# A hybrid transformer block in fp32 on one core: the latent tiles are turned beside the context tiles, and each layer opens with a plain fp32 product by token tile

## The reference, cut to what matters

```python
# first block, second ("odd") layer
h_l = rmsnorm(x, norm_g[l]) * (1 + sc_l[:, None]) + sh_l[:, None]
h_c = rmsnorm(ctx, norm_g[l]) * (1 + sc_c) + sh_c
q, k, v, g = split_cols(h_lat @ w_in, ODD_SPLITS)      # latents only for q and g
ck, cv = split_cols(h_ctx @ w_in[:, GQA_Q:GQA_Q + 2 * GQA_KV], ...)
...
# second block, each of two layers, 256 tokens, D = 1024
u = layer_norm(x) * (1 + sc1) + sh1
proj = u @ w_in + b_in
(p_in, c_b, c_c, c_h, mq, mk, mv, fq, fk, fv, f_logit, gate_logit) = jnp.split(proj, ...)
q_m = apply_partial_rotary(to_heads(mq, MOBA_HEADS), cos, sin)
k_m = apply_partial_rotary(to_heads(mk, MOBA_HEADS), cos, sin)
... # four branches, gates, w_o, layer norm, then the MLP w_up, relu^2, w_down
```

## Time and profile before

| | |
|---|---|
| time, median of 3 runs (range) | 1511.95 us (1504.79 to 1512.63) |
| the profiled execution: its time, its span | 1508.91 us, 1507.1 us |
| mean granted clock of TensorE | 0.955 |
| busy: PE, DVE, ACT, POOL | 90%, 64%, 33%, 10% |
| chain that ended last: PE, DVE, ACT | 74%, 15%, 4% |
| bytes from HBM, mean rate | 255.70 MB, 170 GB/s |

### The profile page before, as it was taken

How to read it: one execution, slowest core, us unless ns; L and a number is a source line. 1 busy time by engine, 2 the same in 40 slices (tenths; PEclk the granted TensorE clock), 3 DMA queues, 4 the chain that set the end, 5 groups by cost and what they waited for, 6 DMA issues and landing times.

```text
span 1507.1 us, 18982 instructions
## 1 busy us (share of the span) xinstructions
PE 1360.5 (90%) x7921; PEld 1115.3 (74%) x7921; DVE 963.0 (64%) x1231; ACT 501.0 (33%) x730; POOL 145.6 (10%) x163
## 2 busy tenths in 40 slices
PE   6999997897997888999998899995999999699996
PEld 1688754543795548888996898984988898598995
DVE  3657464753746875676678766667657677755556
ACT  1322134400434503352332433431453323334431
POOL 2011000100100010001222000001001132000000
PEclk9999999999999998998999899997999999899998
DMA  9353350321640057456565666655556476455551
GB/s 335 142 183 111 117 195 0 112 86 54 225 153 1 1 191 249 155 209 246 209 244 195 214 229 230 221 171 189 167 180 252 152 275 238 131 168 195 169 194 56
DMA packets 104918, 257.97 MB, mean 171 GB/s; under 512 B 8217, under 2 KB 11770, under 8 KB 104578
## 3 DMA queue, kind: packets, MB, share of 16 engines
q1 hardware_dynamic: 80554, 171.78, 33.3%
q0 software_dynamic: 20192, 75.58, 13.8%
q10 hardware_dynamic: 4088, 9.41, 1.9%
HBM read 255.70 MB, written 1.05 MB: 170 GB/s over the span
## 4 chain that ended last, share of the span: by engine, by line
PE 74%; DVE 15%; ACT 4%; issue 3%; ACTq 1%; DMA 1%; POOL 1%; SPq 0%; POOLq 0%; DVEq 0%
PE bank L729 72%; PE bank L875 2%; DVE weights_low L1951 2%; DVE modulation_sums L1769 1%; ACT weights_high L1403 1%; DMA x<-in_ctx_dram 1%; POOL inverse_roots L642 1%; ACT odd_prob L1577 1%; DVE statistics L1911 1%; DVE x L2373 1%; DVE even_A L1896 1%; DVE statistics L1809 1%; DVE x L1910 0%; DVE uT_high L2220 0%; DVE odd_weights_low L1951 0%
## 5 line engine op out<-in xcount | busy, mean ns | idle before, releaser
L1951 DVE TENSOR_TENSOR weights_low<-weight_ring,weights_high 128x2048 fp32r<-128x2048 f32 (+1 forms) x128 | 286.1, 2236 | 283.0 <-ACT weights_high L1403 282.9
L1403 ACT ACTIVATE weights_high<-weight_ring 128x2048 fp32r<-128x2048 f32 (+1 forms) x128 | 238.6, 1865 | 528.6 <-PE bank L729 453.9
L729 PE MATMUL bank<-uT_high,weights_high 128*128 128x256 f32 (+1 forms) x1200 | 346.6, 289 | 7.8 <-DVE weights_low L1951 3.0
L729 PE MATMUL bank<-uT_low,weights_high 128*128 128x256 f32 (+1 forms) x1200 | 344.3, 287 | 0.0
L729 PE MATMUL bank<-uT_high,weights_low 128*128 128x256 f32 (+1 forms) x1200 | 343.9, 287 | 0.0
L729 PEld LDWEIGHTS bank<-uT_high,weights_high 128*128 128x128 f32 (+1 forms) x1200 | 233.7, 195 | 12.8 <-issue 10.1
L729 PEld LDWEIGHTS bank<-uT_low,weights_high 128*128 128x128 f32 (+1 forms) x1200 | 233.7, 195 | 1.0
L729 PEld LDWEIGHTS bank<-uT_high,weights_low 128*128 128x128 f32 (+1 forms) x1200 | 233.6, 195 | 0.5
L1769 DVE SCALAR_TENSOR_TENSOR modulation_sums<-modulation_ring,silu_c_columns,modulation_sums 128x1024 f32<-128x1024 f32 x128 | 175.3, 1369 | 9.9 <-DMA modulation_ring<-in_w_ada_dram 6.9
L729 PE MATMUL bank<-weights_high,hidden_high 128*128 128x512 f32 x256 | 101.7, 397 | 5.2 <-DVE weights_low L1951 5.2
L729 PE MATMUL bank<-weights_low,hidden_high 128*128 128x512 f32 x256 | 101.2, 395 | 0.0
(11 more groups left out here) (287 smaller groups left out, 2168.1 us busy)
## 6 DMA issues: line engine op xcount, KB each, us to landing
weight_ring<-in_w_in_dram SPq DMA_DIRECT2D x52, 1024.0 KB, 6.5
modulation_ring<-in_w_ada_dram POOLq DMA_DIRECT2D x48, 1024.0 KB, 7.4
weight_ring<-in_w_up_dram SPq DMA_DIRECT2D x32, 1024.0 KB, 5.3
weight_ring<-in_w_down_dram SPq DMA_DIRECT2D x32, 1024.0 KB, 4.9
modulation_ring<-in_w_mod_dram POOLq DMA_DIRECT2D x16, 1024.0 KB, 5.4
weight_ring<-in_o_w_in_dram SPq DMA_DIRECT2D x10, 1024.0 KB, 5.1
weight_ring<-in_w_branch_dram SPq DMA_DIRECT2D x16, 512.0 KB, 3.6
weight_ring<-in_w_o_dram SPq DMA_DIRECT2D x8, 1024.0 KB, 6.9
```

The source lines that it names most:

```text
L729: return track(pe.matmul(*args, **kw))
L1403: act.activation(ring[:, s, 0:kn * cols], wring[:, slot, 0:kn * cols], ACT.Copy).then_inc(S["high_ready"], 1)
L1951: dve.tensor_tensor(lo[:, s, 0:kn * cols], wring[:, slot, 0:kn * cols], hi[:, s, 0:kn * cols].bitcast(F32), ALU.subtract).then_inc(w_free[ ...
```

## The change

Names are those of the diff; line numbers in the changed kernel differ by a few.

1. *Even output into odd layer.* A bank now holds two column blocks of one stream (latents or context). PE turns latent tile 0 after output tile 1 and latent tile 1 after output tile 2, all eight column blocks each; the context tiles are turned after `oq0`. DVE scales each tile right after its variance, splits the latent stream after tile 2, makes `oq0,1`, `oq1,0` and `oq1,1` low, then splits the context stream. ACT modulates the context stream after both halves of `oq1`. The temporary of the even output moves to another buffer.
2. *Layer start.* The slab order begins with `in2`, which is no longer split. Each token tile is turned and modulated by itself (8 turns, 8 modulations of 128 columns), and PE multiplies raw fp32 `whole` by raw fp32 `in2`, tile by tile. Then `in0`, `in1`, `in3`, `in4` as before. DVE rotates right after `in0`; in `in3` ACT makes the second half after two bank copies, and DVE puts its modulation product between the halves of `in4`.
3. *Small loads.* Bias rows, selectors, and for the second layer also biases and pool weights, are issued earlier: for the first layer after the odd attention, for the second inside the MLP of the first layer (after `high("up3")`).

```diff
-LAYER_SLABS = (halves("in0", "in1", "in2", "in3", "in4", "forget")
+LAYER_SLABS = (halves("in2", "in0", "in1", "in3", "in4", "forget")
-SPLIT_SLABS = [s for s in LAYER_SLABS if s[0][:6] != "branch"]
+SPLIT_SLABS = [s for s in LAYER_SLABS if s[0][:6] != "branch" and s[0] != "in2"]
-        etmp = E3[:, 0:2 * COLS].rearrange("p (b n) -> p b n", b=2)
+        etmp = acc1[:, 0, :].rearrange("p (b n) -> p b n", b=2)
...  PE, even output into odd layer
             tokens_out_by_tile(both("eout1"), [("eout", 1, i) for i in range(TALL)], eyT_tokens,
-                               between=lambda i: turn_tile(i - 1) if i > 0 else None)
-            turn_tile(TALL - 1)
-            turn_x("oxT", xn_o, range(4, KD), 2 * TALL)
+                               between=lambda i: turn_tile(i - 1, turned) if 1 <= i <= TC else None)
...
+            tokens_out(both("oq0"), [("oq", 0, i) for i in range(TC)], h_tokens, COLS, wait=h_split(0))
+            turned = [start(("oxT", 4 + n)) for n in range(4)]
+            for i in range(TC, TALL):
+                turn_tile(i, turned)
+            tokens_out(both("oq1"), [("oq", 1, i) for i in range(TC)], h_tokens, COLS)
+            tokens_out(both("okv"), [("okv", i) for i in range(TALL)], h_tokens, COLS, wait=h_split(1))
...  PE, layer start
-                turn_xn("xT", 0)
+                def first_tile(o, tt, h):
+
+                    w = slab("in2", h)
+                    copied(("xT", tt, h))
+                    for k in range(4):
+                        ins = product(o[:, :], whole[:, 4 * h + k, P * tt:P * tt + P], w[:, k, :],
+                                      start=(h + k == 0), stop=(h == 1 and k == 3))
...
+                turn_tile(0)
+                firsts = [start(("mqk", tt)) for tt in range(TC)]
+                first_tile(firsts[0], 0, 0)
+                turn_tile(1)
+                first_tile(firsts[0], 0, 1)
+                for h in range(2):
+                    first_tile(firsts[1], 1, h)
-                tokens_out(both("in2"), [("mqk", i) for i in range(TC)], ui, COLS)
...  ACT, even output into odd layer
-            act.wait_ge(S["xn_ready"], 2 * TALL)
-            modulate("oxT", whole_o, (2, 3), range(4))
+            modulate_stream(0)
             high_part("oq0", 1)
-            modulate("oxT", whole_o, (2, 3), range(4, KD))
-            high("oq1", "okv", "og0")
+            high("oq1")
+            modulate_stream(1)
+            high("okv", "og0")
...  ACT, layer start and inside the MLP
+                for tt in range(TC):
+                    for b in range(2):
+                        o = ready(("xT", tt, b))
+                        for n in range(4):
+                            k = 4 * b + n
+                            ins = act.activation(whole[:, k, P * tt:P * tt + P], o[:, P * n:P * n + P], ACT.Identity,
+                                                 bias=mcol[:, 0, k:k + 1], scale=mcol[:, 1, k:k + 1])
+                        release(ins, ("xT", tt, b))
+                    if tt == 0:
+                        act.wait_ge(S["x_out"], sec.at("x_out", 0))
+                        if l == 0:
+                            load_biases(l)
+                high("in0")
+                if l == 0:
+                    load_pools(l)
+                else:
+                    load_pool_matrices()
+                load_norm(l, 1)
...
+                    if j == 2 and not sec.last:
+                        load_rows(l + 1)
+                        load_selectors()
+                        load_biases(l + 1)
+                        load_pools(l + 1)
...  DVE, even output into odd layer
+                normal_o(i)
+                if i == 0:
+                    low("oq0", 0)
+                if i == TC:
+                    split_stream(0)
+            low("oq0", 1)
+            low("oq1")
+            split_stream(1)
...  DVE, first layer start: mod_columns(7, mcol, 1) moved ahead of normal(0, 8)
...  DVE, layer start
-                low("in0", 0)
-                for i in range(4):
-                    copied(("xT", i))
-                    split_u(i)
-                low("in0", 1)
-                low("in1", 0)
+                for tt in range(TC):
+                    for b in range(2):
+                        copied(("xT", tt, b))
+                        src, hi, lo = (v[:, 4 * b:4 * b + 4, P * tt:P * tt + P] for v in (whole, uhigh, ulow))
+                        link(dve.tensor_copy(hi, src))
+                        dve.tensor_tensor(lo, src, hi.bitcast(F32), ALU.subtract).then_inc(S["u_ready"], 1)
+                low("in0")
```

201 lines of the change are left out of this document (113 added, 88 removed).

## The result

Four runs each on the chip: the kernel before took 1512.29 us in the median (1504.79 to 1517.05), the changed kernel 1487.26 us (1481.72 to 1489.12). The ratio is 0.983, with a 95% interval of 0.980 to 0.985. The forecast was 1480 with a range of 1470 to 1494. The profiled execution of the changed kernel took 1481.7 us with a span of 1479.9, against 1508.9 and 1507.1 before: 27.2 us less, where the prediction's sum was 28.9. It was the fastest of the four.

The account below looks back on a forecast made before the run. Three quarters of the chain was PE at work, so only PE's idle, low-clock or needlessly dear stretches counted. From the profiled 1508.9 us, -13 - 7.3 - 9.0 + 0.4 = -28.9 gave 1480 us, range 1470 to 1494.

Parts of the forecast that it names:

- (A): Odd layer: waits for scaled tiles go, two low-part waits come, `okv` begins at 395.5 instead of 408.4, -13 us.
- rival 1: Odd layer: the new pauses of 2.6 and 2.4 us cool the clock, 2.1 us each, 1484 us; chance 0.12.
- (B): First hybrid layer's start: plain products by tile begin at 562.5 instead of 572.7, `in2` falls away later, -7.3 us.
- (C): Second hybrid layer's start: plain products begin at 1035.5, -9.0 us, more than in the first layer since loads stand elsewhere.
- The step that named the fourth half-slab as just in time: First hybrid layer: `in0,1` is low at 585.0, PE wants it at 585.2; nothing to spare, nothing lost.
- The wait at `in4`: Layer starts: PE's wait for DVE before the first `in4` product falls from 1.5 to 0.4 us, -1.1.
- The price of the restart: Layer starts: PE runs 4 us at the low clock after restarting, which loses 2.0 us.
- (D): First layer's MLP: fifteen small loads delay the rounding of `down2,0`, cost 0 to 2.7 us, taken as +0.4.
- The upper bound: First layer's MLP: cost of 2.7 us if the loads start only when the rounding is over.
- Rival 2: Layer starts: the fourth half-slab comes late, 5.7 us more in each layer, 1491 us; chance 0.11.
- Rival 3: Odd layer: each new wait doubles (+5) and the restart cools, odd part -6, 1487 us; chance 0.09.
- Rival 4: Every restart: clock stays low until dense split products come, +16.6 us, 1525 us; chance 0.04.

Follow-up runs that it names:

- odd part alone: The kernel before with only the odd layer's part of the change, layer starts and small loads as they were: 1499.7 us, ratio 0.992.
- six traces: Traces of six kernels that have the changed kernel's code at the second layer's start, which took 90.3 to 92.1 us, 91.4 in the mean.
- the second trace: The changed kernel measured again, unaltered, beside the others on one chip: 1488.7 us, ratio 0.983.
- the experiment: The changed kernel with the last two half products of tile 1 swapped, so `in2,0` stays in use 3.4 us longer: 1496.7 us (1 run).
- loads alone: The kernel before with only its small loads moved off the layer starts, ten still ahead of the first layer's modulation: 1503.6 us, ratio 0.994.
- `oq0,1` edit: The changed kernel with the low part of `oq0,1` made on DVE ahead of the last tile's normalisation: 1489.1 us (1 run).
- four edits: The changed kernel with `okv,0` and `oq0,1` low parts earlier, MLP loads spread, second layer's tile 0 normalised earlier: 1476.5 us, ratio 0.976.
- layer part alone: The changed kernel with the odd layer's part taken back to what it was: 1498.5 us, ratio 0.991.
- `in2` split: The changed kernel with the first product by token tile done in three split passes instead of plain: 1497.3 us, ratio 0.990.

## Why the prediction came out as it did

**(A) Odd layer, -13 forecast; `okv` began 10.7 us earlier (11.1 counted from the output product).** The steps held: the waits for `odd_xn` went, and two for the low parts came, forecast 2.6 and 2.4, measured 2.36 and 3.12. From the end of `oq0,1` on (381.7) DVE's queue ran as forecast: low part of `oq1,1`, four splits, rotations, low part of `okv,0`. PE was 0.3 us quicker than forecast over its turns and two half-slabs, and starts 0.25 after the low part ends, so the second wait is longer. What was missing is the clock, at 1.7 us for the one low stretch of that trace; rival 1 had put 2.1 on each pause. The odd part alone, whose clock did not fall before `okv`, began that block 12.6 us earlier than before, counted the same way: the 12.9 of the forecast. The gain itself is not clock: on the chain 1.7 us were lost to it before and 1.7 after, and the 11 us are waits and work.

**(B) -7.3 forecast, -7.4 from `okv` to the first scores (-7.6 from the last output product); (C) -9.0 forecast, -8.8, or -7.7 by the mean of six traces.** (B) had the right size; (C) came as near only in the shortest trace, and the forecast is 1.3 us too high against the mean. The step that named the fourth half-slab as just in time was right to the tenth. The forecast start of the first product, 562.5 less 12.9, gives 549.6; it was 551.7, as (A) was short by 2.2. The wait at `in4` went altogether, where 0.4 was forecast. The low clock at the first restart lay on 5 us of plain products, not 4. The forecast did not say which part earns how much; the loads and the order by tile turned out nearly equal. Why (C) exceeds (B) was put down to the loads: they do give 1.3 us more there, but what is left over besides loads and order gives 1.2 less, and by the mean (C) hardly exceeds (B).

The price of the restart was right, but its reason was misread. The prediction took the low clock after 572.7 for what the sixteen turns at 564 had left as it was. The clock had in fact risen at 566.6, and fell again at 570.0, while PE waited 4.2 us for the split (the row of the turns, then windows):

```profile
563.89 3.25 PE L875 MATMUL bank<-constants,xn 128*128 128x128 f32 x16
564.00:566.00 2.00, 2.00 (x11) 2.00 (x11) 1.91 (x3) 1.09 (x1) 1.71 (x3) 0.50 0.89 364
566.00:567.00 1.00, 1.00 (x8) 0.90 (x6) 1.00 (x1) 0.00 (x0) 0.91 (x2) 0.70 0.61 150
569.00:570.00 1.00, 0.00 (x0) 0.00 (x0) 0.00 (x0) 0.00 (x0) 0.00 (x0) 1.00 0.92 282
570.00:571.00 1.00, 0.00 (x0) 0.00 (x0) 0.00 (x0) 0.62 (x2) 0.00 (x0) 0.51 1.00 381
```

**(D) +0.4 forecast, +0.8 measured,** and 0.1 in the second trace. The fifteen issues took 7.5 us (7.7 forecast, from 9.75 us over 19 loads; the trace of before has 18). The upper bound, in which they start only when the rounding is over, does not occur: the first went out 0.01 us after the rounding began.

**The sum** was made against one profiled execution, 3 us under the median then shown, and came out 1.7 us from the profiled execution of the changed kernel. That it is so near is partly luck: (A) fell 2.2 us short, and the profiled execution was the fastest of its four. Medians are 25.0 apart, not 27.2 or 28.9. The last 2.7 us of the traces' difference lie in the second layer's gate phases, which the change does not touch: there the clock was lower in the trace of before than in that of after. The same two blocks of branch products took 25.04 us at a mean clock of 0.86 and 20.29 at 0.83 in the kernel before. In the changed kernel:

```profile
1127.48:1151.09 23.61, 23.61 (x155) 20.18 (x154) 13.10 (x20) 8.35 (x18) 2.91 (x4) 0.93 0.54 201
1151.74:1170.57 18.83, 18.83 (x136) 17.43 (x136) 13.52 (x19) 4.22 (x11) 3.97 (x4) 0.91 0.68 251
```

In the first layer it went the other way: 197.2 against 195.7. This is chance, not an effect of the change.

One thing the sum had no term for: over whole runs the low clock shrank. A run's time multiplied by 1 less its mean granted clock is 73.9 us in the mean of eleven runs of the kernel before and 62.0 in six of the changed one, 11.9 us less of some 25. A part of it falls where PE waits or is off the chain, and lengthens nothing.

**The rivals.** *Rival 1* (the pauses cool the clock) is what happened, by half in the first trace and whole in the second, at 1.7 us each. *Rival 2* (the slab late) did not happen in the first trace; its premise, no slack, is shown by the experiment, and its price was set too low, for the clock comes on top. In four other traces the second layer's slab landed in 5.5 to 6.5 us and PE waited 0.5 to 1.6 us for it; in three a later slab took some 13 us beside ACT's 2 MB of constants and norm rows, for a wait of 0.5 to 0.8. *Rival 3* (DVE holds back the odd layer) fell: the pauses were not twice as long. *Rival 4* (the clock stays low until dense split products come) fell. The clock was back at 1.0 by 557, under the plain products of tile 0:

```profile
551.00:553.00 2.00, 1.28 (x2) 0.79 (x3) 1.91 (x5) 1.98 (x6) 0.18 (x1) 0.50 0.43 103
...
555.00:557.00 2.00, 2.00 (x4) 0.82 (x3) 1.93 (x4) 0.00 (x0) 1.56 (x3) 0.57 0.23 35
557.00:559.00 2.00, 2.00 (x12) 1.26 (x11) 0.86 (x2) 0.65 (x2) 0.00 (x0) 1.00 0.92 309
```

The turns of tile 1 at 557.71 did not bring the low clock back. The rule that the prediction took from the Trainium skill ("TensorE: Matmul & The Clock Gate", Part 4: PE-mode transpose) says that turns do not bring the full clock as other work does. The kernel before shows otherwise: there the clock rose at 566.6, when PE had done one product of one column (from 563.44) and then only turns (from 563.89). It rose likewise under the sixteen turns in the odd part alone (at 560.7) and in *loads alone* (at 574.2).

## What to carry to other kernels

Where a stage starts with operands that must be prepared on two engines, look for one product that can run on what is there already, in a dearer form: here 16 plain fp32 products took 2.9 us more than 48 split ones and opened an order worth some 3.2 at each start, because they need neither rounded weights nor the second token tile. Small loads at a stage start are worth moving by themselves: taking 8 of 18 issues in the first layer and 15 in the second off ACT's queue there gave 3.4 and 4.7 us. And when a wait goes, read the queue of the engine that releases the next one: two moves on DVE's queue alone, seen only in the new trace, took a further 5 us.

## What the runs showed of the hardware

**The length of a pause did not decide whether the clock fell.** The pause before `oq0,1` (2.3 to 2.4 us) stood in eight traces; behind it PEclk fell to 0.5 in five. The one before `okv,0` (3.1 to 3.2 us) stood in eight; the clock fell behind it in six. In five traces it fell behind one of the two alone. Of nine pauses of 3.53 us in the three kernels that keep the odd layer of before, seven went with a fall. A low stretch of the odd layer took away 1.7 us of full clock each time, or 3.4 where it lasted twice as long (less where PE was waiting anyway), and could begin inside dense products behind pauses of 0.7 and 0.95 us alone, as near 341 us in the kernel with the `oq0,1` edit and in the one with all four. An expected gain from "no pause, no low clock" is therefore an average, and one trace is a poor witness for it; the means of six runs each, 62.0 us lost in the changed kernel and 56.9 with the four edits, are a better one.

**The spread of whole runs is largely this.** The gate phases of layer 1 took 191.4 to 198.8 us in thirteen traces of the same code; in two at the ends of that range (the layer part alone and `in2` split), the clock's loss, counted as in the ledger, was 9.4 and 17.0 us. Of seventeen runs of the kernel before, the fastest took 1505.4 us at a mean clock of 0.956, the slowest 1517.9 at 0.948: 66 and 79 us less full clock.

**A sequencer issues loads while its engine computes.** Fifteen issues began 0.01 us after a rounding of 1.92 us did, took 7.5 us, and held back only the next rounding. A pool-weight issue took 0.77 us (3.09 for four), the others 0.27 to 0.48.

**The clock rises behind turns.** Three traces show it at the first layer's start, at 566.6, 560.7 and 574.2 us, behind up to sixteen turns with one product of one column ahead of them.
